# A fused decoder layer: order of work at its stage and block borders, a second up weight split early, and the last down halves in up's buffers

## What is computed

```python
h = rms_norm(x, pre_mix_norm)
proj = h @ w_in                        # 1024 -> 2304 columns
y_rwkv = rwkv7_group(proj[..., :1792], ...)    # 8 heads of 64, state recurrence over time
y_pool = multiscale_pool(proj[..., 1792:], w_pool, pool_scale)   # windows 2, 4, 8, 16
mixed = concatenate([y_rwkv, y_pool]) @ w_out
x = x + rms_norm(mixed, post_mix_norm)
h = rms_norm(x, pre_ffn_norm)
up = causal_depthwise_conv3(h @ w_up) + conv_b          # 1024 -> 2 * 2816
gate, val = split(up)
x = x + rms_norm((gelu(gate) * val) @ w_down, post_ffn_norm)
```

## Time and profile before

| | |
|---|---|
| median of three runs | 2601.85 us (2597.11 to 2603.88) |
| the profiled execution | 2603.83 us, of which the span of the trace is 2601.9 us |
| TensorE busy | 2447.2 us, 94% of the span; mean granted clock 0.973 of full speed |
| VectorE, ScalarE, GpSimd busy | 62%, 45%, 18% |
| projection | 0 to about 570 us |
| recurrence | about 570 to 885 us |
| output projection | about 885 to 1115 us |
| FFN | about 1115 us to the end; three block borders at about 1525, 1895 and 2264 us |

### The profile page before, as it was taken

The page is one execution under the profiler, slowest core; times in us unless marked ns, Lnnn a source line. Parts: engine busy times, 40 slices in busy tenths (PEclk is TensorE's granted clock), DMA queues, the critical chain, the costliest instruction groups (busy, mean ns, idle before and its releaser), DMA issues. The chain is left out here.

```text
span 2601.9 us, 43203 instructions
## 1 busy us (share of the span) xinstructions
PE 2447.2 (94%) x16932; PEld 1988.2 (76%) x16932; DVE 1612.1 (62%) x1925; ACT 1170.7 (45%) x1823; POOL 479.0 (18%) x396
## 2 busy tenths in 40 slices
PE   6999999968999599979999999999999999999997
PEld 4777767647888488768888878888878888788886
DVE  2766797945865454456666666666676666666666
ACT  4656564523444345444444444444534444444443
POOL 4646464532333434300000000000000000000000
PEclk9999999988999799989999999999999999999999
DMA  6373735345676357853333543334443334333322
GB/s 175 96 227 113 227 122 187 122 162 137 168 185 158 103 180 227 263 180 97 97 97 97 194 125 92 92 94 143 148 129 93 92 92 158 114 97 97 97 81 81
DMA packets 488076, 353.98 MB, mean 136 GB/s; under 512 B 72396, under 2 KB 438396, under 8 KB 487420
## 3 DMA queue, kind: packets, MB, share of 16 engines
q1 hardware_dynamic: 429116, 293.24, 37.9%
q10 hardware_dynamic: 58816, 58.73, 6.8%
HBM read 272.21 MB, written 79.69 MB: 135 GB/s over the span
## 5 line engine op out<-in xcount | busy, mean ns | idle before, releaser
L2250 DVE TENSOR_TENSOR p_acc<-late_bank,p_acc 128x512 f32<-128x512 f32 x320 | 221.1, 691 | 194.9 <-PE late_bank L125 184.2
L123 PE MATMUL late_bank<-p_dn_hi,p_a_hi 128*128 128x512 f32 x704 | 282.1, 401 | 18.0 <-DVE p_acc L2247 12.6
L2220 DVE SCALAR_TENSOR_TENSOR p_cv<-p_ub,p_cpar,p_cv 128x512 f32<-128x512 f32 x176 | 127.6, 746 | 252.5 <-ACT p_cv L2135 252.5
L124 PE MATMUL late_bank<-p_dn_lo,p_a_hi 128*128 128x512 f32 x704 | 281.6, 400 | 0.0
L125 PE MATMUL late_bank<-p_dn_hi,p_a_lo 128*128 128x512 f32 x704 | 281.3, 400 | 0.0
L123 PE MATMUL p_ppr<-p_hT_hi,p_w_hi 128*128 128x512 f32 x576 | 234.8, 408 | 0.4 <-DVE p_hT_lo L670 0.2
L397 POOL TENSOR_TENSOR p_w_lo<-p_w_raw,p_w_hi 128x1024 fp32r<-128x1024 f32 x72 | 184.7, 2565 | 239.4 <-ACT p_w_hi L465 239.4
L124 PE MATMUL p_ppr<-p_hT_lo,p_w_hi 128*128 128x512 f32 x576 | 227.5, 395 | 0.0
L125 PE MATMUL p_ppr<-p_hT_hi,p_w_lo 128*128 128x512 f32 x576 | 227.2, 394 | 0.0
L2124 ACT ACTIVATE p_ub<-late_bank 128x1024 f32<-128x1024 f32 x88 | 90.3, 1026 | 272.1 <-PE late_bank L125 265.7
L2146 ACT ACTIVATE p_a_hi<-p_cv 128x512 fp32r<-128x512 f32 x88 | 55.6, 632 | 339.0 <-DVE p_cv L2230 339.0
(11 more groups left out here) (256 smaller groups left out, 5710.2 us busy)
## 6 DMA issues: line engine op xcount, KB each, us to landing
first_up_raw<-in_w_up SPq DMA_DIRECT2D x176, 512.0 KB, 5.0
p_dn_raw<-in_w_down SPq DMA_DIRECT2D x88, 512.0 KB, 4.2
p_w_raw<-in_w_in SPq DMA_DIRECT2D x72, 512.0 KB, 3.9
x_block<-in_x SPq DMA_DIRECT2D x8, 1024.0 KB, 6.7
p_x<-in_x SPq DMA_DIRECT2D x16, 512.0 KB, 5.1
scratch_x<-p_x ACTq DMA_DIRECT2D x16, 512.0 KB, 2.8
scratch_h_hi<-p_h_hi ACTq DMA_DIRECT2D x16, 512.0 KB, 5.8
scratch_h_lo<-p_h_lo ACTq DMA_DIRECT2D x16, 512.0 KB, 4.5
```

What stands on the lines that cost most here:

```text
L123: nc.tensor.matmul(out, lhs_hi, rhs_hi, start=start, stop=False)
L124: nc.tensor.matmul(out, lhs_hi, rhs_lo, start=False, stop=False)
L2220: nc.vector.scalar_tensor_tensor(cv[s][:, i, :], ub[s][:, i, 1:1 + TB], cpar[s][:, i, 1:2], cv[s][:, i, :], ALU.mult, ALU.add).then_inc(s_ ...
L2250: nc.vector.tensor_tensor(dst, bank[:, 4 + n % 4, :], dst, ALU.add).then_inc(s_acc, 1)
```

## The change

At the end of the projection, the last block's pooling works in the buffers of V (`vA`, `vB` in `um`) and waits for the turned V and the bonus product instead of the stored bonus; TensorE and ScalarE do the first pair of pool products ahead of the rows of a, and the pooled tiles are stored by two DMAs of 512 KB, one for each pair, with one more wait of SP. In the recurrence, the loads of the gram matrix and of the mask "above" go ahead of the twelve small loads of the inverses. In the output projection, ScalarE and VectorE also split the second up weight behind the last high half, ahead of ScalarE's last two stores of low halves; its halves lie in the memory of `w_lo`. In the FFN, TensorE turns the taps between the two halves of the second up product. In the group g = 1 of a block, VectorE's output tiles 2 and 3 stand between the sums of the new block. In the very last group ScalarE makes the high halves of the down weights ahead of gelu, VectorE does the four taps of slot 1 together, two sums, the low halves, the product left over and then four sums; the last down halves go to the buffers of the up weight (`dn_tile`).

```diff
         eps = sb("eps", [P, 1])
         sA = tmp[:, 0:2, :].rearrange("p a t -> p (a t)")[:, 0:HALO + TB]
         sB = tmp[:, 2:4, :].rearrange("p a t -> p (a t)")[:, 0:HALO + TB]
+
+        vA = um[:, V0:V0 + 2, :].rearrange("p a t -> p (a t)")[:, 0:HALO + TB]
+        vB = um[:, V0 + 2:V0 + 4, :].rearrange("p a t -> p (a t)")[:, 0:HALO + TB]
...
                 for s in (s_gst, s_pst, s_rst, s_kst, s_bst, s_atst, s_btst):
                     sp.wait_ge(s, ONE + 16 * BLOCKS)
+                sp.wait_ge(s_pst, ONE + 16 * BLOCKS + 16)
...
                     last.then_inc(s_pout, 1)
-                    if r == 1:
+                    if b == BLOCKS - 1:
+
+                        act.wait_ge(s_pout, ONE + b * 2 + r + 1)
+                        g = POOL_GROUP[2 * r + 1]
+                        act.dma_start(scr["mix"][:, PAIRS + g:PAIRS + g + 2, bass.ds(b * TB, TB)], gate[:, g:g + 2, :]).then_inc(s_pst, 16)
+                    elif r == 1:
                         act.wait_ge(s_pout, ONE + b * 2 + 2)
                         act.dma_start(scr["mix"][:, PAIRS:2 * PAIRS, bass.ds(b * TB, TB)], gate[:, :, :]).then_inc(s_pst, 16)
...
                 read_ab(BLOCKS - 1)
+                pool_out(BLOCKS - 1, 0, [pm[:, 2, :], pm[:, 3, :]])
                 a_rows(BLOCKS - 1, LAST)
-                pool_out(BLOCKS - 1, 0, [pm[:, 2, :], pm[:, 3, :]])
                 pool_out(BLOCKS - 1, 1, [pm[:, 0, :], pm[:, 1, :]])
...
                 def pool(b, x):
 
                     g = POOL_GROUP[x]
+                    last = b == BLOCKS - 1
+                    if x == 0 and last:
+
+                        dve.wait_ge(s_vt, ONE + b + 1)
+                        dve.wait_ge(s_bo, ONE + b + 1)
+                    if x == 0 and not last:
+                        dve.wait_ge(s_bst, ONE + b * 16 + 16)
                     if x == 0:
-                        dve.wait_ge(s_bst, ONE + b * 16 + 16)
                         dve.wait_ge(s_at, ONE + b + 1)
                         dve.wait_ge(s_plm, ONE + b * 2)
...
-                    src, dst, other = u, sA, sB
+                    src, dst, other = u, *((vA, vB) if last else (sA, sB))
...
                 pe.wait_ge(s_prf, ONE + BLOCKS * FT)
+                pool_products(BLOCKS - 1, 0, [pm[:, 2, :], pm[:, 3, :]])
                 rows(dec, LAST, s_atn)
-                pool_products(BLOCKS - 1, 0, [pm[:, 2, :], pm[:, 3, :]])
                 pe.wait_ge(s_abr, ONE + BLOCKS)
                 pool_products(BLOCKS - 1, 1, [pm[:, 0, :], pm[:, 1, :]])
...
                     if i == -1:
+                        load_ab(FIRST)
+                        sp.dma_start(above[:, :, :], const_view(a, "above")).then_inc(s_ab, 16)
                         for n in range(1, BATCH):
                             sp.wait_ge(s_xz[n], ONE + 1)
                             spread(n)
-                        load_ab(FIRST)
-                        sp.dma_start(above[:, :, :], const_view(a, "above")).then_inc(s_ab, 16)
...
         w_hi = sb("w_hi", [P, KT, D_MODEL], F32R)
-        w_lo = sb("w_lo", [P, KT, D_MODEL], F32R)
+        w_lo = scr["w_lo"]
...
                 high_h(N - 1, 1)
+                act.wait_ge(s_up1, ONE + 32)
+                nc.scalar.activation(scr["up_hi"][1][:, :, :, :], scr["up_raw"][1][:, :, :, :], ACT.Copy).then_inc(s_uh, 1)
                 store_low(N - 2, 0)
                 store_low(N - 1, 1)
...
                 tiles(nc.vector, body, ahead)
                 turn(N - 1, 1)
+                dve.wait_ge(s_uh, ONE + 2)
+                nc.vector.tensor_tensor(scr["up_lo"][1][:, :, :, :], scr["up_raw"][1][:, :, :, :], scr["up_hi"][1][:, :, :, :].bitcast(F32),
+                                        ALU.subtract)
...
-        hT_hi = [scr["hT"][0], sb("hT_hi1", [P, KT, TB], F32R)]
...
-        up_hi = [scr["up_hi"], sb("up_hi1", [P, 2, KT, P], F32R)]
-        up_lo = [scr["up_lo"], sb("up_lo1", [P, 2, KT, P], F32R)]
+        up_hi = scr["up_hi"]
+        up_lo = scr["up_lo"]
...
+        def dn_tile(tiles, own, b, g, s):
+
+            if isinstance(g, int) and b == BLOCKS - 1 and g == GROUPS - 1:
+                return own[s][:, :, :, :].rearrange("p i k n -> p (i k n)")[:, 0:D_MODEL]
+            return tiles[s][:, :]
...
                     before = preceding(b, g)
-                    if before:
+                    if isinstance(g, int) and b == BLOCKS - 1 and g == GROUPS - 1:
+                        act.wait_ge(s_upd, ONE + BLOCKS * FF)
+                    elif before:
                         act.wait_ge(s_db, ONE + before[1] * BANKS + (before[0] * GROUPS * BANKS + BANKS))
...
                         taps(b, g, s)
                         if after:
                             high_up(*after, s)
+                        if isinstance(g, int) and b == BLOCKS - 1 and g == GROUPS - 1 and s == GROUP - 1:
+                            high_dns(b, g)
                         gelu(b, g, s)
                         high_a(b, g, s, p)
-                act.sem_inc(s_uh, 1)
-                act.wait_ge(s_uh, ONE + 1)
-                high_up(0, 0, 1)
+
+                act.sem_inc(s_uh, GROUP)
+                act.wait_ge(s_uh, ONE + GROUP)
                 act.wait_ge(s_const, ONE + 1)
                 act.wait_ge(s_cw, ONE + 1)
                 stream(nc.scalar, group)
-                high_dns(BLOCKS - 1, GROUPS - 1)
                 norm_last(BLOCKS - 1)
...
                 def low_dn(b, g, s):
                     dve.wait_ge(s_dh, ONE + at(b, g, s) + 1)
-                    nc.vector.tensor_tensor(dn_lo[s][:, :], dn_raw[s][:, :], dn_hi[s][:, :].bitcast(F32),
+                    nc.vector.tensor_tensor(dn_tile(dn_lo, up_lo, b, g, s), dn_raw[s][:, :], dn_tile(dn_hi, up_hi, b, g, s).bitcast(F32),
                                             ALU.subtract).then_inc(s_dl, 1)
...
-                dve.sem_inc(s_ul, 1)
-                dve.wait_ge(s_ul, ONE + 1)
-                low_up(0, 0, 1)
+                dve.sem_inc(s_ul, GROUP)
+                dve.wait_ge(s_ul, ONE + GROUP)
                 dve.wait_ge(s_cwt, ONE + 1)
                 nc.vector.tensor_copy(cw[:, :, :, :], cw_bank).then_inc(s_cw, 1)
                 dve.wait_ge(s_par, ONE + 16 * NPAR)
...
                     hidden(b, g, 0)
                     low_a(b, g, 0, p)
                     if last:
-                        output(b - 1, (2, 3))
-                        dve.wait_ge(s_fin, ONE + b * TT)
+                        dve.wait_ge(s_fin, ONE + b * TT - 2)
                     add_down(before, (0, 1))
                     dve.wait_ge(s_tap, ONE + at(b, g, 1) + 1)
+                    if isinstance(g, int) and b == BLOCKS - 1 and g == GROUPS - 1:
+
+                        tap1(b, g, 1, 0)
+                        tap1(b, g, 1, 1)
+                        tap0(b, g, 1, 0)
+                        tap0(b, g, 1, 1).then_inc(s_cv, 1)
+                        add_down(before, (2, 3))
+                        low_dns(b, g)
+                        leftover(b, g, p)
+                        add_down(before, (4, 5, 6, 7))
+                        return
                     tap1(b, g, 1, 0)
                     add_down(before, (2,))
                     tap1(b, g, 1, 1)
                     add_down(before, (3,))
+                    if last:
+                        output(b - 1, (2,))
+                        dve.wait_ge(s_fin, ONE + b * TT - 1)
                     tap0(b, g, 1, 0)
                     add_down(before, (4,))
                     tap0(b, g, 1, 1).then_inc(s_cv, 1)
-                    add_down(before, (5, 6, 7))
+                    add_down(before, (5,))
+                    if last:
+                        output(b - 1, (3,))
+                        dve.wait_ge(s_fin, ONE + b * TT)
+                    add_down(before, (6, 7))
 
                 stream(nc.vector, group)
-                leftover(BLOCKS - 1, GROUPS - 1, (BLOCKS * GROUPS - 1) % 2)
-                low_dns(BLOCKS - 1, GROUPS - 1)
...
                     for i in range(2):
+                        if isinstance(n, int) and n == 1 and i == 1:
+
+                            pe.wait_ge(s_par, ONE + 16 * NPAR)
+                            for tap in range(TAPS):
+                                last = nc.tensor.transpose(bank[:, 4, tap * 2 * FF:(tap + 1) * 2 * FF], cw_rows[:, tap, :],
+                                                           ident[0:2 * FF, 0:2 * FF])
+                            last.then_inc(s_cwt, 1)
                         for k in range(KT):
...
+                            hi, lo = dn_tile(dn_hi, up_hi, b, g, s), dn_tile(dn_lo, up_lo, b, g, s)
                             last = split_matmul(nc, bank[:, 4 + n % 4, :], a_hi[p][s][:, t * P:(t + 1) * P], a_lo[p][s][:, t * P:(t + 1) * P],
-                                                dn_hi[s][:, h * TB:(h + 1) * TB], dn_lo[s][:, h * TB:(h + 1) * TB],
+                                                hi[:, h * TB:(h + 1) * TB], lo[:, h * TB:(h + 1) * TB],
```

(11 more changed lines are left out.)

11 lines of the change are left out of this document (5 added, 6 removed).

## The result

The changed kernel takes 2568.37 us (median of six runs, 2564.29 to 2574.69) against 2602.41 us for the kernel before in runs beside it: a ratio of 0.9875, 95% interval 0.9860 to 0.9891. The prediction said 2567. The profiled execution took 2568.12 us with a span of 2566.3 us, 35.6 us less than the span before; the mean granted clock is 0.98.

What follows compares the result with a forecast made beforehand. TensorE, busy nearly the whole span, was taken as the bound, so its standing still was attacked. Terms 19.2 + 6.5 + 6.8 + 1.6 + 0.6 = 34.7 us off the profiled 2603.83 gave 2569.1, median 2567 us; range 2560 to 2579.

Steps and rivals of the forecast that it cites:

- the fourth row of the budget: Stretch from the recurrence's first state product of step i = 1 to the FFN's start: forecast gain -0.8 us.
- later end of the stage: Output projection ahead of the FFN: splitting the second up weight delays its last stores, costing 0.8 us (0.3 to 1.8).
- Block borders: Three FFN block borders: reordered VectorE work removes TensorE's stalls and the half clock behind them, 19.2 us (16.8 at least).
- margin of 0.8 us: Block borders: smallest time by which VectorE frees a bank before TensorE needs it, so TensorE doesn't wait.
- Rival (b): Borders still stall: VectorE's chain 3.3 us later than laid out, 14.4 us lost, 2581 us; chance 0.09.
- Rival (c): Borders: up loads behind the delayed store land too late, kernel slower than before, 2614 us at 36 us landing; chance 0.03.
- Rival (d): VectorE's order matters nowhere, stalls move to the next bank; only recurrence and projection gain, 8.4 us, 2593; chance 0.04.
- Tail: Last group: TensorE starts the last down products sooner, idle 1.25 us instead of 5.43, clock stays full; gain 6.5 us.
- rival (a): New waits replace removed ones: clock falls in the tail (4.1), k lands late in the recurrence (4.5); 2572 us; chance 0.22.
- Start of the recurrence: Reordered loads remove VectorE's 5.50 us wait for the mask, TensorE goes on sooner at full clock; 6.8 us (4.5 to 7.5).
- End of the projection: Last block's pooling starts early instead of awaiting the stored bonus, last store issued sooner; 1.6 us (0.5 to 2.8).
- Start of the FFN: TensorE's 14.75 us wait for the gain goes, but nearly all becomes a new 2.9 us wait; 0.6 us (-1.5 to 3.2).

Runs made afterwards that it cites:

- borders_undone: Changed kernel with VectorE making output tiles 2 and 3 ahead of the new block's first sum again at all three borders: 2588.82 us, ratio 0.9933 to before.
- tail_order_undone: Changed kernel with VectorE's old order in the last group, ScalarE's high halves still early: 2576.28 us (one run).
- all_together: both_waits_out plus old projection-end order with free second pool pair and split store, last norm's gain loaded later and awaited at first block border: 2565.74 us, ratio 0.9849.
- pool_start_alone: Kernel before with only the last block's pooling in V's buffers, old order of rows and one 1 MB store: 2602.83 us, ratio 1.0001.
- taps_earlier: Changed kernel with last norm's gain on its own semaphore and taps turned behind 12 matmuls of the second up product, not 24: 2569.12 us, ratio 0.9856.
- both_waits_out: taps_earlier plus another VectorE order in the last group, fifth sum ahead of the second down weight's low half: 2564.91 us, ratio 0.9851.
- mask_load_alone: Kernel before with only the gram matrix and mask loads moved ahead of the twelve small loads of the inverses: 2599.73 us, ratio 0.9992.

## Why the prediction was right

**Total.** 2567 against 2568.4, each gain where it was placed, no term off by more than 1.5 us. The total owes something to luck: the recurrence gave 1.5 us less than forecast, the end of the projection and the start of the FFN 0.6 and 0.7 more, and the profiled execution began 1.0 us ahead by scatter. That the fourth row of the budget (-0.6) meets its forecast (-0.8) is chance, since the later end of the stage that was meant there did not occur.

**Block borders: right**, 19.2 against 18.9, and 18.0 by taking the edit back. The margin of 0.8 us was real: moving tile 2 ahead of two taps and two banks (2.5 us of work) gave 1.7 us of waiting, so 0.8 had been free. Rival (b) needed a VectorE chain 3.3 us late; it was on time to 0.1 us. Rival (c) didn't occur: SP issues the next up loads at 1527.13, behind the delayed store, and the readings behind the border keep their period. Rival (d) is refuted by borders_undone.

**Tail: right**, 6.5 against 6.55. The idle time was 1.19 us; the prediction's 1.25 does not follow from its own times, by which TensorE would stand from 2578.18 - 5.43 = 2572.75 to 2573.85, 1.1 us. That the clock stays full held. The reasons given for it were weaker than they looked: the waits from 1.7 us up were not all alike in the trace of before (behind 2.29 us ahead of 557.62 the clock was 1.00 until 562.5), and the 1.68 us of the earlier trace rows bring half clock in some executions and not in others. With twice the idle time rival (a)'s half in the tail did occur once; its price was 1.5 us, not 2.4.

**Start of the recurrence: the wait right, the sum 1.5 us too high.** The step i = 0 took 14.9 us instead of 21.4, which is 6.5 of the 6.8 forecast. The missing 1.2 us lie ahead of it, in a place that the prediction put at nothing and did not look at: the first state product of i = 0 came 28.47 us behind the stage's start, before 27.31. Two things are in that. GpSimd's copies of b and k ahead of that product, for which TensorE waits, began 15.88 us behind the start (582.96 above), before 15.04 (585.34); both times a load of k released them. That is 0.84 us. The rest, 0.3 us, goes with the clock. Over the first 29 us of the stage the granted clock was 0.58 on the mean, before 0.66. The 14 traces fall into two sets: seven with 0.66 or 0.67, in which the first state product comes 27.3 to 27.6 us behind the start, and seven with 0.58 to 0.63, in which it comes after 27.8 to 29.0. The first set has all five kernels without the whole of the projection's edits and also two with them (borders_undone, tail_order_undone); the second has all_together, whose end of the projection keeps the old order. So neither part of the projection's edits is shown to be the cause. Why k lands later and the full clock comes later is open.

**End of the projection: size nearly right (1.6, measured 2.2 to 2.3), reason incomplete.** The step that failed is the one unsaid: the prediction gave the gain to the early pooling, with the order of the rows as a consequence. pool_start_alone shows that TensorE's wait for ScalarE's reading of the first pair, hidden before, would have taken the whole of it. The gain beyond 1.6 is an issue 0.4 us sooner than laid out and a landing 0.2 us shorter: 9.16 us from the last issue to the next stage against 9.40. The profile gives the two halves of 512 KB landings of 3.1 and 3.7 us, where the 1 MB store had 4.0. The last half, which counts, is the one of 3.7: nearer to my 4.0 than to 3.2, the estimate from the Trainium skill ("DMA: Bandwidth & Descriptors", Anatomy of one DMA). The difference has a place: in every trace with two halves, the half that is issued right behind the store of the rows of a lands after 3.7 us (in all_together that is the first half), the other after 2.7 to 3.5. Both are faster than the 512 KB stores of h in the earlier trace rows, at 4.2 to 4.9. In all 14 traces the recurrence starts 5.4 to 5.5 us behind the landing of the last store, while from its issue it is 8.6 to 9.4, so the stage's end follows that landing.

**Start of the FFN: the mechanism right, 2.1 (with an undelayed end of the stage before) against 0.6.** The new wait came as forecast, 2.93 us for 2.9, and half clock behind it: from 1123.51 to the third reading it is 12.79 us, 1.9 more than the 10.93 counted for full clock (forecast 2.3). Two terms were mis-sized. The later end of the stage (0.8) was nothing: ScalarE's queue issued the store beside the split, the last issue fell on the end of GpSimd's last low half as before, and from the start of that low half to the next stage it is 10.43 us, before 10.42. And the half clock at the start lasted 3.1 us from TensorE's first matmul, not 3.5 to 5.5, which keeps the first reading at 8.54 us behind the start (8.49 before) instead of 0.45 later. The wait for the gain was gone only in name: the turn comes 7.46 us behind the start, before 7.37. The edit pays through the 24 matmuls that TensorE does meanwhile.

## What to carry to other kernels

A long wait that ends last in a stretch is not the stretch's price: ask which wait stands right behind it, and pair the edits (here early pooling with a free second pair, early split with a later turn). Of the halves that were run alone, the early pooling and the early split were worth nothing and the new order at the projection's end cost 0.9 us. Where a stall at a border comes from one engine's order, lay out that engine's instructions against the times at which the stalled one needs each buffer; here this gave the gain of the borders to 1.2 us of 19.2 and the next stall to 0.1 us. A change of a few microseconds in a kernel whose stages scatter by more is measured between marks in the trace.

## What was not expected of the hardware

- **Idle time and clock.** Idle times of 1.19, 1.70 (three times) and 2.32 us within the FFN were followed by full clock, full clock, and half clock for 3.4 us that began 1.4 us after the restart. One and the same wait of 1.68 us in the projection was followed by half clock in eight traces (in before 1.1 us after the restart) and by full clock in six. Idle time alone does not decide, and a single row of before is no forecast for the same place in the next execution; what else decides is open.
- **Half clock behind a stage's start varies.** From the first matmul of the FFN's start to the thirteenth it was 4.3 us in the changed kernel; the turn behind the same 12 came after 5.4 us in taps_earlier and after 4.7 us in both_waits_out. The Trainium skill ("TensorE: Matmul & The Clock Gate", Part 1) says that the point at which the clock rises differs between executions of one kernel; these rows, of kernels whose program is the same up to there, agree.
- **The recurrence's length.** With the old load order it took 316.6 to 330.0 us in four executions, with the new one 311.2 to 316.8 in ten. The removed wait is 6.4 us; the rest is scatter and spells of half clock (0.88 and 0.84 in two windows of 42 us of pool_start_alone, 1.00 and 0.92 in those of mask_load_alone), which I can't attribute.
- **VectorE beside GpSimd.** The pooling's first additions at 534.86 took 2.40 us for three where the same three took 2.17 us later in the trace of before; GpSimd was making copies beside them, as in the trace of pool_start_alone (2.40 as well).
